# Attention products split into high and low parts, score order rewritten, bank drains moved ahead of ring waits

## The reference, cut to what matters

```python
s1 = einsum('bqhd,bkhd->bhqk', qa, k1) * scale          # differential attention, two maps a head
s2 = einsum('bqhd,bkhd->bhqk', qb, k2) * scale
a = causal_softmax(s1, i, S) - lam * causal_softmax(s2, i, S)
o = einsum('bhqk,bkhe->bqhe', a, v)                      # v is 256 wide
...
s = (einsum('bqhd,bkhd->bhqk', qn, k_nope)               # MLA: 128 wide, plus
     + einsum('bqhr,bkr->bhqk', qr, k_rope)) * scale     # 64 rotary wide, k_rope shared by the heads
p = causal_softmax(s, i, S)
o = einsum('bhqk,bkhd->bqhd', p, v)
```

## Time and profile before

| what | before |
|---|---|
| median of 3 runs | 2063.18 us (2062.92 to 2064.4) |
| the profiled execution, its own time | 2063.65 us |
| its span, first to last instruction | 2061.9 us |
| TensorE busy | 2051.7 us, 100% of the span |
| VectorE busy | 1194.4 us, 58% |
| ScalarE busy | 989.3 us, 48% |
| granted TensorE clock | 0.999 of full |
| differential attention, TensorE's attention pieces | about 28 to 320 us |
| MLA pairs | about 1145 to 1275 us |

### The profile page before, as it was taken

One profiled execution on the slowest core, in us unless ns is written; L12 is line 12 of the kernel. 1 busy time (PEld: TensorE's weight loads), 2 busy tenths in 40 slices (PEclk: granted clock), 3 DMA queues, 4 the chain that ended last, 5 costly groups with the idle time before them and its releaser, 6 DMA issues.

```text
span 2061.9 us, 28683 instructions
## 1 busy us (share of the span) xinstructions
PE 2051.7 (100%) x10470; PEld 1761.2 (85%) x10470; DVE 1194.4 (58%) x1474; ACT 989.3 (48%) x1360; POOL 10.1 (0%) x22
## 2 busy tenths in 40 slices
PE   9999999999999999999999999999999999999998
PEld 7888888888888888888888998888888888888887
DVE  7655555565556556555655666566556556655655
ACT  7554555444345334434446665544434434434443
POOL 0000000000000000000000000000000000000000
PEclk9999999999999999999999999999999999999999
DMA  7655545665665665556555444575666556656653
GB/s 278 239 164 169 177 161 166 190 196 186 194 193 176 207 187 184 202 183 190 196 184 164 136 131 146 187 218 184 198 190 183 200 186 183 202 187 181 203 186 120
DMA packets 261129, 381.76 MB, mean 185 GB/s; under 512 B 8785, under 2 KB 145233, under 8 KB 260945
## 3 DMA queue, kind: packets, MB, share of 16 engines
q1 hardware_dynamic: 260352, 378.90, 57.3%
q10 hardware_dynamic: 720, 2.10, 0.3%
HBM read 378.87 MB, written 2.10 MB: 185 GB/s over the span
## 4 chain that ended last, share of the span: by engine, by line
PE 84%; issue 15%; DVE 0%; POOL 0%; ACT 0%; POOLq 0%; DVEq 0%
PE acc L470 23%; PE acc L441 15%; PE acc L443 15%; PE acc L442 15%; PE acc L480 12%; PE side L505 1%; PE side L785 0%; PE side L784 0%; PE acc L751 0%; PE acc L759 0%; PE acc L760 0%; PE acc L761 0%; PE acc L752 0%; PE acc L753 0%; PE side L795 0%
## 5 line engine op out<-in xcount | busy, mean ns | idle before, releaser
L1289 DVE TENSOR_TENSOR wlo<-raw,whi 128x1024 fp32r<-128x1024 f32 (+1 forms) x700 | 840.3, 1213 | 663.5 <-ACT whi L879 661.7
L879 ACT ACTIVATE whi<-raw 128x1024 fp32r<-128x1024 f32 (+1 forms) x700 | 726.2, 1051 | 727.8 <-PE acc L443 479.4
L441 PE MATMUL acc<-whi,opB 128*128 128x512 f32 x1264 | 493.4, 390 | 0.0
L443 PE MATMUL acc<-whi,opB 128*128 128x512 f32 x1264 | 491.9, 389 | 0.0
L442 PE MATMUL acc<-wlo,opB 128*128 128x512 f32 x1264 | 491.8, 389 | 0.0
L470 PE MATMUL acc<-opA,whi 128*128 128x512 f32 x2048 | 478.2, 390 | 0.0
L470 PEld LDWEIGHTS acc<-opA,whi 128*128 128x128 f32 x2048 | 380.3, 188 | 76.2
L443 PEld LDWEIGHTS acc<-whi,opB 128*128 128x128 f32 x1264 | 237.2, 188 | 49.5
L441 PEld LDWEIGHTS acc<-whi,opB 128*128 128x128 f32 x1264 | 237.3, 188 | 48.7
L442 PEld LDWEIGHTS acc<-wlo,opB 128*128 128x128 f32 x1264 | 237.3, 188 | 48.7
L480 PEld LDWEIGHTS acc<-opA,wlo 128*128 128x128 f32 x2048 | 254.2, 192 | 5.0
(11 more groups left out here) (203 smaller groups left out, 986.0 us busy)
## 6 DMA issues: line engine op xcount, KB each, us to landing
raw<-in_w_up SPq DMA_DIRECT2D x128, 1024.0 KB, 5.8
raw<-in_w_down SPq DMA_DIRECT2D x128, 1024.0 KB, 5.0
raw<-in_a_w_qkv SPq DMA_DIRECT2D x44, 1024.0 KB, 5.1
raw<-in_a_w_o SPq DMA_DIRECT2D x16, 1024.0 KB, 5.0
raw<-in_b_w_o SPq DMA_DIRECT2D x16, 1024.0 KB, 5.0
raw<-in_w_ukv SPq DMA_DIRECT2D x8, 1024.0 KB, 5.5
raw<-in_b_w_uq SPq DMA_DIRECT2D x8, 576.0 KB, 4.0
raw<-in_w_dkv SPq DMA_DIRECT2D x4, 1024.0 KB, 5.1
```

The lines of the kernel that those rows point to most:

```text
L441: mm(o, a_hi, w_hi, start=first and c == 0, stop=False)
L443: done = mm(o, a_lo, w_hi, start=False, stop=last and c == chunks - 1)
L879: done = fn(whi[:, place:place + ch, 0:n], raw[:, r, c0:c0 + ch, 0:n], ACT.Copy)
L1289: done = tt_(wlo[:, place:place + ch, 0:n], raw[:, r, c0:c0 + ch, 0:n], whi[:, place:place + ch, 0:n].bitcast(F32), ALU.subtract)
```

## The change

1. In differential attention, scores of 256 columns and all value products become three float32r products each, as high and low parts. Scores of 128 columns stay float32. The four 128-column scores come first, then the 256-column ones map by map. ACT writes the high parts from the PSUM banks; DVE subtracts for the low ones (`q_low`, `k_low`, `da_attnT_lo`, `v_lo`).
2. V is drained by ACT (high) and then DVE (`v_lo`, scaled subtract), and it is DVE's pass that now frees the bank of `acc[0]`.
3. In MLA the 256-column parts of scores are split likewise. The rotary part holds high and low rows of q stacked in 128 partitions, and takes two float32r products against `kr_hi` and `kr_lo`. `mla_values(p-2)` moves ahead of K/V half 2.
4. In the urgent blocks, halves 0 and 1 and halves 6 and 7 run token tile by token tile over both halves (`two_halves`), so that bank 0 is finished 12 products ahead of the block's end. The drains of ACT, and the rotary work and `v_lo` of DVE, stand ahead of the split of the next block's half 2.
5. The first pair's q transposes move to after half 1 of its v block, its k drain and rotation to after half 6 of that block's splits, `x_sum_squares` from half 1 to half 2. The gains come by a DMA of their own on ACT's queue ahead of the first weights. The x of the first norm lies in `xs`, whose reload waits for `x_sums`.
6. Buffers are shared differently, and the last norm's gain multiplies one block later.

```diff
@@ TensorE @@
+            def two_halves(b, hf, s, op, first=False, last=False, uses=0):
+                for t in range(TT):
+                    for h in range(2):
+                        pe.wait_ge(lo_ready, 8 * b + hf + h + 1)
+                        for c in range(2):
...
+                            if start:
+                                wait_bank(s, uses, t)
...
+                            if end and t == 0:
+                                done.then_inc(bank0_done, 1)
+                done.then_inc(pe_halves, 2)
             def da_scores(p, first=False):
-                pe.wait_ge(qkT_ready, 4 * p + 4)
+                pe.wait_ge(qkT_lo, 2 * p + 2)
...
                 for m in range(4):
-                    mm(side[m][:, 0:P], qT[:, m, 0:P], kT[:, m, 0:P], start=True, stop=True)
-                    mm(side[m][:, P:KEYS], qT[:, m, P:SEQ], kT[:, m, :], start=True,
-                       stop=True).then_inc(scores_done, 1)
+                    mm(side[m][:, 0:P], q_first[:, m, :], k_first[:, m, :], start=True, stop=True)
+                for m in range(4):
+                    o = side[m][:, P:KEYS]
+                    mm(o, q_hi[:, m, :], k_hi[:, m, :], start=True, stop=False)
+                    mm(o, q_hi[:, m, :], k_lo[:, m, :], start=False, stop=False)
+                    mm(o, q_lo[:, m, :], k_hi[:, m, :], start=False, stop=True).then_inc(scores_done, 1)
...
-            def mla_scores(p):
+            def mla_scores(p, par):
...
-                for h in range(2):
-                    bank = side[3 * (1 - h)]
-                    for q0, q1, k1, o0, o1 in ((0, P, P, 0, P), (P, SEQ, SEQ, P, KEYS)):
-                        mm(bank[:, o0:o1], qh[:, h, q0:q1], kh[:, h, 0:k1], start=True, stop=False)
-                        done = mm(bank[:, o0:o1], qr[:, q0:q1], krz[:, h, 0:k1], start=False, stop=True)
-                    done.then_inc(scores_done, 1)
+                for h in range(2):
+                    mm(side[3 * (1 - h)][:, 0:P], q_first[:, h, :], k_first[:, 2 * par + h, :], start=True, stop=False)
+                for h in range(2):
+                    o = side[3 * (1 - h)][:, 0:P]
+                    mm(o, qr[:, h, 0:P], kr_hi[:, 0:P], start=False, stop=False)
+                    mm(o, qr[:, h, 0:P], kr_lo[:, 0:P], start=False, stop=True)
+                for h in range(2):
+                    o, k = side[3 * (1 - h)][:, P:KEYS], 2 * par + h
+                    mm(o, qm_hi[:, h, :], k_hi[:, k, :], start=True, stop=False)
+                    mm(o, qm_hi[:, h, :], k_lo[:, k, :], start=False, stop=False)
+                    mm(o, qm_lo[:, h, :], k_hi[:, k, :], start=False, stop=False)
+                    mm(o, qr[:, h, P:SEQ], kr_hi, start=False, stop=False)
+                    mm(o, qr[:, h, P:SEQ], kr_lo, start=False, stop=True).then_inc(scores_done, 1)
@@ mla_pair, TensorE @@
                     mla_transposes(p - 1)
...
+                if prev2:
+                    mla_values(p - 2, u)
                 half_kv(b, 4 * u + 1, ckvT[2:4], False, U_MLA[1] + p)
...
-                    mla_scores(p - 1)
-                if prev2:
-                    mla_values(p - 2, u)
+                    mla_scores(p - 1, 1 - u)
@@ ScalarE @@
+            act.dma_start(gains[:], gains_x[:, 0:G_PAD]).then_inc(gains_in, 16)
             act.dma_start(raw[:, 0, 0, :], W_QKV[:, 0, 0:NB]).then_inc(chunk_in[0], 16)
...
+            def drain_v(b):
+                act.wait_ge(bank0_done, b + 1)
+                for t in range(TT):
+                    if t:
+                        used(b)
+                    fn(v_hl[:, 0, t, :], acc[0][:, t, :], ACT.Copy, scale=rs[:, 0, t:t + 1]).then_inc(v_hi, 1)
...
             def mla_drain_kv(b, hf, par):
-                act.wait_ge(pe_halves, 8 * b + hf + 1)
...
+                act.wait_ge(pe_halves, 8 * b + hf)
+                keys = acc[1][:, 0, :].rearrange("p (h t) -> p h t", h=2)
+                fn(k_hi[:, 2 * par:2 * par + 2, :], keys, ACT.Copy).then_inc(k_ready, 1)
+                fn(k_first[:, 2 * par:2 * par + 2, :], keys[:, :, 0:P], ACT.Copy).then_inc(k_ready, 1)
+                fn(v_mla[:, par], acc[1][:, 1, :].rearrange("p (t n) -> p t n", t=TT), ACT.Copy).then_inc(drained[1], 1)
...
                 split(nb, h0, nxt)
+                mla_drain_kv(b, 4 * u + 2, u)
                 if prev:
                     mla_exps(p - 1)
@@ VectorE @@
+            def v_lo(p):
+                for t in range(TT):
+                    dve.wait_ge(v_hi, TT * p + t + 1)
+                    stt(out=v_hl[:, 1, t, :], in0=acc[0][:, t, :], scalar=rs[:, 0, t:t + 1],
+                        in1=v_hl[:, 0, t, :].bitcast(F32), op0=ALU.mult, op1=ALU.subtract).then_inc(drained[0], 1)
...
+                asides.update({6: first_rope_k if first else lambda: k_low(p), 8: lambda: da_softmax(p, (0, 1)),
+                               9: lambda: da_softmax(p, (2, 3))})
+                body(b + 2, asides, end=10)
+                v_lo(p)
+                split(b + 3, 2)
...
                 split(b, 4 * u + 3, "mla")
+                if prev:
+                    mla_q_lo(p - 1)
                 split(nb, h0, nxt)
+                mla_k_lo(p, u)
                 if prev:
                     mla_softmax(p - 1)
                     mla_weights(p - 1)
```

More of the change, by code:

```diff
@@ L223, in trunk @@
         x_in = sem("x_in")
+        gains_in = sem("gains_in")
         xT_first = sem("xT_first")
@@ L344, in _ @@
             qkv(0, True)
+            sp.wait_ge(x_sums, 5)
             for j in range(JB):
@@ L432, in half_tok @@
                 order = [(c, t) for c in range(chunks) for t in range(TT)]
-                if urgent and (first or last):
+                if by_tile:
                     order = [(c, t) for t in range(TT) for c in range(chunks)]
@@ L454, in block_tok @@
                         ready(hf)
-                    half_tok(b, hf, s, chunks_of(buf, 2 * hf), n, first=hf == 0, last=hf == 7, uses=uses,
-                             urgent=urgent)
+                    if urgent and hf in (0, 6):
+                        two_halves(b, hf, s, chunks_of(buf, 2 * hf, 4), first=hf == 0, last=hf == 6, uses=uses)
+                    elif not (urgent and hf in (1, 7)):
+                        half_tok(b, hf, s, chunks_of(buf, 2 * hf), n, first=hf == 0, last=hf == 7, uses=uses)
                     if aside and hf in aside:
@@ L880, in split, with body @@
                 done.then_inc(hi_ready, 1)
-            def body(b, asides=None, kind=None, nxt=None):
-                for hf in range(3, 11):
+            def body(b, asides=None, kind=None, nxt=None, end=11):
+                for hf in range(3, end):
                     if hf < 8:
@@ L1531, in qkv @@
                 else:
-                    body(b, {4: lambda: da_weights(pv)})
-                if not first:
+                    body(b, {4: lambda: da_weights(pv)}, end=10)
                     rope_qk(p, 0)
-                def stats_and_angles():
-                    first_stats()
-                    angles()
+                    split(b + 1, 2)
                 def lambda_and_rope():
@@ L1621, in mlp @@
                         asides[4] = lambda: x_lo(v_out + j - 1, None)
+                    if l == 1 and j:
+                        asides[4] = lambda: with_norm_weight(j - 1)
                     if l == 1 and j == JB - 1:
@@ L1682, in mla_weights, with mla_q_lo, mla_k_lo @@
                             ALU.mult).then_inc(attn_ready, 1)
+            def mla_q_lo(p):
+                dve.wait_ge(qkT_ready, 2 * DA_PAIRS + 2 * p + 1)
+                tt_(qm_lo, both(0, 1)[:, :, P:SEQ], qm_hi.bitcast(F32), ALU.subtract).then_inc(qkT_lo, 1)
+                dve.wait_ge(qkT_ready, 2 * DA_PAIRS + 2 * p + 2)
+                for h in range(2):
+                    own, other = (slice(ROPE * k, ROPE * k + ROPE) for k in (h, 1 - h))
+                    done = tt_(qr[other, h, :], side[2][own, 0:SEQ], qr[own, h, :].bitcast(F32), ALU.subtract)
+                done.then_inc(qkT_lo, 1)
+            def mla_k_lo(p, par):
+                dve.wait_ge(k_ready, 2 * p + 2)
+                tt_(k_lo[:, 2 * par:2 * par + 2, :], acc[1][:, 0, :].rearrange("p (h t) -> p h t", h=2),
+                    k_hi[:, 2 * par:2 * par + 2, :].bitcast(F32), ALU.subtract).then_inc(drained[1], 1)
             def mla_lo(p):
```

283 lines of the change are left out of this document (171 added, 112 removed).

## The result

| | before | changed |
|---|---|---|
| median, same chips | 2063.49 us (13 runs) | 2068.42 us (2068.11 to 2071.45, 13 runs) |
| ratio | 1 | 1.0025 (95%: 1.0016 to 1.0033) |
| span of the profiled execution | 2061.9 us | 2066.6 us |
| granted TensorE clock | 0.999 | 0.999 |

The account below looks back on a forecast made before the run. TensorE, busy 2051.7 of 2061.9 us, was taken as the bound, so products removed and new waits count fully. Terms -3.8 + 8.7 + 3.0 + 0.1 + 0.4 = +8.4 gave 2071.6 us, range 2063 to 2076.

Parts of the forecast that it names:

- part A: TensorE's products in differential attention and MLA: splitting them into float32r saves 3.8 us.
- the signs that the prediction set for itself: Forecast wrong if weight transposes don't idle, 128-column float32r products don't cost 0.22 us, or `v_lo` starts before TensorE's block ends.
- A second sign: At the V bank: the prediction is wrong if `v_lo` starts before TensorE ends its block.
- the cheap price: Alternative lower price of a 128-column float32r product, 0.12 us instead of 0.22; the sum is then +5.8 us.
- B, weights wait: MLA weight transposes wait, since moved values leave less cover and the chain lengthens: +8.7 us over seven pairs.
- C, V bank: Differential attention: the next pair's q block waits 1.0 us for `v_lo` at three transitions, +3.0 us.
- D, first pair: First pair: the wait for the sum of squares goes, -1.1 us; the k transposes wait, +1.2.
- E, small ones: Gains' DMA taken at 0.2 us and `kr_lo` at 0.2; weight ring, `x_sums` and last norm nothing: +0.4.
- 0.2 us of room: MLA: slack left to rotated q and copied weights before the next pair's transposes, given no cost.
- (1): Rival, faster: chains stay under cover, the weights chain at most 5.6 us; 2058.3 us, or 2055 cheap; chance 0.1.
- (2): Rival, about the same: 128-column products cheap and no V bank wait; +2.8 us, 2066; chance 0.17.
- (3): Rival, slower still: rotated q or copied weights late in MLA, 1 us more in six pairs; 2078; chance 0.13.

Follow-up runs that it names:

- v_low_early: Changed kernel with VectorE's pass on V bank 0 put ahead of the softmax's last quarter: 2065.44 us, ratio 1.0011.
- k_late_only: Changed kernel with only VectorE's MLA k subtraction moved behind the softmax's bias, score products in the change's order: 2068.45 us, one run.
- k_late_head_first: Changed kernel with VectorE's MLA k subtraction moved behind the softmax's bias and all of head 0's score products done first: 2065.29 us, ratio 1.0010.
- values_back: Changed kernel with the MLA values put back behind the scores, and V's drain with them: 2062.14 us, ratio 0.9995.
- old_values_ahead: Kernel before the change with one move, MLA values ahead of K/V half 2: 2069.71 us, ratio 1.0031.
- old_ahead_kv_now: Kernel before with MLA values ahead, ScalarE's K/V drain ahead of the exponentials and allowed once K/V half 2 is done, separate key rows: 2067.30 us, ratio 1.0019.
- all_but_gains: Changed kernel with values back, k subtraction late, head 0 first, V bank 0 pass and first k drain early; gains still loaded first: 2056.16 us, ratio 0.9964.
- one_half: Changed kernel with urgent blocks run half by half again, without `two_halves`: 2068.12 us, ratio 1.0023.
- all_covered: Changed kernel with values back, k subtraction late, head 0 first, V bank 0 pass and first k drain early, old order of first loads: 2056.35 us, ratio 0.9966.

## Why the prediction came out as it did

**Right: the side, the two mechanisms and their places.** It was predicted that the weight transposes of MLA wait in 7 pairs (they do, 6.7 by the list, where 7 to 10 was given), that the first q products of pairs 1 to 3 wait for `v_lo` with 3.0 in all (shown by v_low_early: 3.0), and that both come from work on VectorE and ScalarE that is no longer covered. The 6.7 lies just under the 7 to 10 given. The range held the time, but it was wide: the point in it, 2071.6, was 3.2 too high, and the MLA pair, given as 15.3 to 15.4, took 14.88 and in two cases 15.17.

**The term that was mis-sized: the price of a float32r product of 128 columns, in part A.** The prediction took 0.22 us, because the float32 product of that shape was the nearest row. It took 0.11 to 0.14, close to what the transposes in the earlier trace rows showed as the lower end. A pair's scores are 2.08, not 2.52. By the signs that the prediction set for itself, this one came true: in this term it was wrong. A second sign missed by little: `v_lo` started at 77.77, and TensorE ended its block at 77.50 + 0.23 = 77.73. Term by term, measured by distances between the same events:

| term | predicted | with the cheap price | measured |
|---|---|---|---|
| A, work of TensorE | -3.8 | -7.0 | 4 x -0.75 in differential attention, 8 x -0.54 in MLA: -7.3 |
| B, weights wait | +8.7 | +9.3 | six pairs +5.25 and their 3.24 of work saved: 8.5; first +0.7: +9.2 |
| C, V bank | +3.0 | +3.0 | a pair 74.25 to 74.33 instead of 74.04, with 0.75 saved, x 3: +3.0 |
| D, first pair | +0.1 | +0.1 | with E, up to the first scores: -0.1 |
| E, small ones | +0.4 | +0.4 | between the layers: -0.2 |
| sum | +8.4 | +5.8 | +4.7 in the span |

With the cheap price the forecast would have been 2069.0, against 2068.4. A part of that nearness is luck. The version before ran 0.3 slower beside the change (2063.49) than in the runs that the forecast started from (2063.18), and with the cheap price A is off by 0.3, B by 0.1, D and E together by 0.8. The sum hung on this one price, although only 32 products have it: the 32 x 0.11 = 3.5 us that they save count fully, while the cover they take away adds just 0.5 to the wait, because the chain gets shorter by most of it too.

**B, the chain.** By the cheap case the mask add came 1.8 after the scores' start, behind VectorE's k subtraction; it came at 1.71, the weights at 6.73 and the next pair's products at 7.08, 0.35 behind them. The prediction took 0.49 for this from the earlier trace rows, by the second product's row less 0.12; the first product's own row starts 0.39 behind the weights (1168.26):

```profile
1168.65 0.38 PE L751 MATMUL acc<-opB,whi 128*128 128x256 f32 x1
```

Its 0.65 for the passage was read in the same way and is 0.57 by the first row. Both readings are 0.1 too long, and they cancel in the wait. k_late_only shows that head 0's last product ends within 0.03 of the k subtraction, and k_late_head_first what both together are worth. That values are the cover is shown by values_back, in the changed kernel, and by old_values_ahead, in the old one. What the prediction didn't see is the second wait in the chain: it wrote that the transposes have 0.2 us of room behind the shifted chain "and lose a drain of K/V that stood before them". In the old kernel that drain costs 2.4 us where it was (old_values_ahead against old_ahead_kv_now), and the change moved it. This was right, but was argued in half a sentence and not priced.

**C.** `v_lo` was expected 7.90 us after the scores' start and came at 77.77 - 69.93 = 7.84. The steps of the sum came in within 0.15 us: the mask add at 1.46 for 1.44, the softmax 6.38 long for 6.46, the first product into the bank at 8.63 for 8.77.

**D and E.** The wait for the sum went, and that at the k transposes came with 0.97 for 1.2. The small terms of E, taken at 0.4, don't show: all_but_gains has no cost for the order of the loads, and one_half none for the tile order. `kr_lo` has no run of its own; it lies in the stretch between differential attention and MLA, which got 0.2 us shorter. There the kernel before has a wait at the first q half of MLA that the change's list doesn't have:

```profile
PE acc L441 <- DVE opA L1649: 0.2, 1, 0.2
```

Why it is gone was not tested.

**The rivals.** (1) needed both chains under cover. It is false for the change and becomes true in all_covered: 2056.35, where 2055 was given for it with the cheap price. (2) had the right price of 128 columns but no V wait, and the V wait was there (2.1 in the list, 3.0 by v_low_early). (3) did not occur in the change; the rotated q and the copied weights never held the transposes.

## What to carry to other kernels

On a kernel whose first engine never rests, look first for what an instruction covers, then for what it costs: as cover for a chain on two other engines, the values product (1.31 us long) was worth 1.0 us a pair in the changed kernel (15.0 on average with it moved, 13.94 with it back) and 0.6 in the old one. When a drain or a wait is moved, compare its new place with the event it counts, and not only with its queue: the same two copies cost 23 us or saved 2.4 by which half they waited for. When two things end within 0.1 us of each other ahead of a link, an experiment that removes one of them can show nothing (k_late_only), so remove both before you call either free.

## What the runs showed of the hardware

- A float32r product costs 0.11 to 0.14 us with 128 columns and 0.12 with 256 (timeline of TensorE above), while a float32 product of 128 columns costs 0.22. So, by an estimate from these rows, three float32r products of 128 columns would take 0.33 or more, longer than one in float32, and at 256 columns 0.36 is less than 0.435. Two, as for the stacked rotary rows, take about as long as one float32 product did (0.26 and 0.22 in the timeline above). The Trainium skill (TensorE: Matmul & The Clock Gate, back-to-back issue gap) puts an isolated 128-column product at 128 / 2.4 + 2.5 = 56 ns. It says in the same place that this counts too little at few columns, and that about 81 ns were measured for a stream with a weight load before each product. The rows here show 110 ns and more, so they decide.
- A wait costs more than its own row in the list of waits: 6.7 us for the weights there, 9.2 by the distances between pairs. The rest lies in the passage behind it (0.76 for 0.57), in the idle time of a row, which is 0.95 where the sum of the work gives 1.11, and in the loop's turn, which shows as an idle time of the weight loads put down to issue (timeline of the change, the next pair).

```profile
1227.60 1.01 PE L608 MATMUL side<-ident,attn 128*128 128x128 f32 x6 [0.95 <-DVE attn L1803]
...
1228.63 0.19 PEld L790 LDWEIGHTS acc<-opB,whi 128*128 128x128 f32 x1 [0.27 <-issue]
1228.64 0.38 PE L790 MATMUL acc<-opB,whi 128*128 128x256 f32 x1
```
